# Delta rule in packed 32x32 blocks for all chunks at once, differential attention kept in flight, fox tails last

## The chip, the cores and the metric

The kernel runs on one core of a Trainium2 chip. The metric is the device time of one execution in microseconds (us): the median of three runs. One more execution was taken by the hardware profiler; all rows below are of that one. The engines are PE (TensorE, the matrix engine; PEld is its weight load), DVE (VectorE), ACT (ScalarE), POOL (GpSimd) and SP (SyncE, which only issues transfers). Each has its own instruction queue and works through it in order; they wait for each other by semaphores. PE reads SBUF and writes PSUM, which has 8 banks of 128x512 numbers. Everything is computed in 32-bit floats; a 32-bit matmul appears in the trace as two PE instructions, a transpose as one.

## The reference, cut to what matters

Four layers on 512 tokens (528 with 16 meta tokens) of width 1024: an even layer (pooling and differential attention), an odd layer (latent attention and the gated delta rule), a forgetting ("fox") attention with a mixture of experts, and a gated recurrence ("hg") with a second mixture of experts. The change touches three of them.

```python
def diff_attention(q, k, v, lam):            # 6 heads, two maps of depth 64 each, causal
    s = einsum('bqhmd,bkhmd->bhmqk', qb, k) * scale
    pr = softmax(where(mask, s, -inf))
    a = pr[:, :, 0] - lam * pr[:, :, 1]
    return einsum('bhqk,bkhe->bqhe', a, v)   # then rmsnorm(o, subln) * (1 - lam_init) * silu(b_gate)

dq = l2norm(dq) * DK_D ** -0.5; dk = l2norm(dk)          # 4 heads of 128
def gated_delta_rule(q, k, v, g, beta):
    gc = cumsum(g)                                        # inside each chunk
    gamma = exp(where(incl, gc[..., :, None] - gc[..., None, :], -inf))
    a_mat = eye + where(strict, (k @ k.T) * gamma * beta[..., :, None], 0)
    u, w = triangular_solve(a_mat, [v * beta, k * beta * exp(gc)])
    qk = (q @ k.T) * gamma
    for each chunk:                                       # S is 128x128 per head
        v_new = u - w @ S
        o = (q * exp(gc)) @ S + qk @ v_new
        S = S * exp(gc_last) + (k * exp(gc_last - gc)).T @ v_new

# fox attention: 16 heads of 64; scores plus differences of cumulated forget gates, causal, softmax, times v
```

## The kernel before

The program is a chain of stages, each a block in which every engine has its own list; an engine enters the next block when its own list is done and the others are. Where this text names a line as L373, it is that line of the kernel; L373 is the helper `products`, which records a sum of matmuls for many stages.

**Even input** (`stage_even_in`): PE makes 36 units of eight matmuls, ACT and DVE empty the banks, POOL rotates the heads.

**Even attention** (`stage_even_attention`): 24 jobs (t, h), four query tiles t of 128 by six heads. A job has keys of width 128(t+1). PE makes two maps of scores (L780, depth 64) and adds the causal mask to each by a matmul with the identity (L781); DVE takes the row maximum (L880) and scales it (L882); ACT takes the exponential out of PSUM with its sum (L844); DVE inverts the sums, scales the first map (L893) and adds the second (L895); PE transposes the result (L789), ACT copies it (L835), PE multiplies it by the values (L373), DVE copies that out (L903). Scores of job j+1 stand ahead of the transposes of job j, and have to wait until the exponentials of job j-1 have read their bank. After six heads DVE squares, sums, normalises and gates the row tile (L908 to L916), with the root on POOL (L279, L281, L283), and PE turns it (L805). The pooling of the even layer (POOL L710 to L731, two matmuls, DVE L745) stands in the same stage.

**Odd input** (`stage_odd_in`): units of eight matmuls in the order low, cgate, conv (12), small (8 columns), dgate. DVE makes the convolution of each conv unit (L1048 to L1053), ACT its silu (L1019).

**Delta rule** (`stage_delta`): first a block that transposes all twelve channel groups (L1387), takes the norms of queries and keys per token on DVE and POOL (L1446 to L1450) and turns them back (L1396), then makes the log gates. Then a second block goes over four chunks of 128 tokens, one after the other, each with its four heads side by side: masks and decays (L1628 to L1640), then the inverse of the unit triangular matrix by doubling: at levels 1 to 6 PE makes L*T (L1531), DVE copies it (L1647), PE makes U*X and X*U (L1537, L1540), DVE masks the next level (L1650) and subtracts (L1654, L1658); T and U are the inverse and its transpose, 128x128 for each head. Then the scan step (L1546 to L1563), and for each chunk a root and two products on POOL (L1609, L1611) and a transpose (L1517).

**Fox attention** (`stage_fox_attention`): jobs of one list; first four "tail" jobs (four heads each, 16 queries), then 32 "pair" jobs (two heads, query tile t). PE: scores (L1926, L1928; for tails L1917, L1918), then the transposes of the job three back (L1944; L1938, L1940), then the products of the job four back (L1965; L1956, L1957). DVE adds the gate row and takes the minimum in one instruction (L2038), ACT takes the exponential in place (L1998), POOL scales by the inverted sum (L2016). SP loads gate rows for later jobs and then zeroes the expert rows in memory (`zero_expert_rows`).

`inverse_root` (POOL L275 to L283) serves all norms. `stage_hg` builds its 32x32 masks from the constants by 24 small copies (L3016), and multiplies blocks of 32 columns (L2712).

## Time and profile before

| | us |
|---|---|
| median of three runs | 3334.73 (3331.75 to 3338.49) |
| profiled execution, its own time | 3341.96 |
| its span, first to last instruction | 3340.1 |
| PE busy | 2668.4 (80%) |
| DVE busy | 871.8 (26%) |
| ACT busy | 498.9 (15%) |
| POOL busy | 448.6 (13%) |
| even attention, 232.5 to 426.3 | 193.8 |
| odd input, 599 to 754.5 | 155.5 |
| delta rule, 895.5 to 1123.4 | 227.9 |
| fox attention, 1472.0 to 1598.1 | 126.1 |

The span is that of the instructions; 1.9 us of the execution's time lie around it. Busy shares are averages over stages that are bound by different things. PE is busy in four fifths of the span, but a busy matmul record is not a full array: the records overlap and their ends are modelled. What counts is the distance between starts. "PEclk" is the share of 2.4 GHz that was granted; 0.50 means 1.2 GHz.

### The profile page before, as it was taken

How to read it: one execution, taken by the hardware profiler on the slowest of the kernel's cores; microseconds unless marked ns; L12 is line 12 of the kernel's file. 1: busy time of each engine (PE TensorE's matmuls, PEld its weight loads, DVE VectorE, ACT ScalarE, POOL GpSimd, SP SyncE). 2: the span in 40 equal slices, each digit the busy share in tenths (PEclk: the TensorE clock that was granted, in tenths of full speed). 3: DMA queues.
4: the chain of work that ended last, by engine and by line, in shares of the span. 5: the costliest groups of instructions: out<-in, count | busy, mean ns of one | idle time of the engine just before them, and what ended most of it. 6: DMA issues, size and time to landing. Idle time of an engine off the chain costs nothing. (4 is left out here: it accounts for less than half of the span.)

```text
span 3340.1 us, 31732 instructions
## 1 busy us (share of the span) xinstructions
PE 2668.4 (80%) x12346; PEld 1339.6 (40%) x12346; DVE 871.8 (26%) x1847; ACT 498.9 (15%) x1154; POOL 448.6 (13%) x681
## 2 busy tenths in 40 slices
PE   6988888995757898999838777775989875777774
PEld 3654444452556544456432222222435442222221
DVE  2315411124366213205131110103055422101111
ACT  1102101012300002115100000001134300000000
POOL 1510001006010002217110000002044200000001
PEclk9995599997778999989959999997989887998987
DMA  4220012102000004203349999995101035999997
GB/s 148 76 91 1 0 54 76 51 16 91 1 1 1 26 8 147 76 8 120 143 195 367 416 415 417 415 416 172 36 27 52 26 153 220 415 417 415 416 415 289
DMA packets 196225, 570.13 MB, mean 171 GB/s; under 512 B 21040, under 2 KB 31152, under 8 KB 195984
## 3 DMA queue, kind: packets, MB, share of 16 engines
q1 hardware_dynamic: 181136, 534.77, 41.0%
q0 software_dynamic: 4736, 17.04, 1.4%
q10 hardware_dynamic: 10240, 16.79, 1.4%
q8 instruction: 74, 1.21, 0.1%
q14 instruction: 39, 0.32, 0.0%
HBM read 524.23 MB, written 44.21 MB: 170 GB/s over the span
## 5 line engine op out<-in xcount | busy, mean ns | idle before, releaser
L373 PE MATMUL psum<-weight_ring,hidden_T 128*128 128x512 f32 (+3 forms) x1792 | 714.1, 557 | 14.5 <-DMA arena<-in_p_T 10.4
L373 PEld LDWEIGHTS psum<-weight_ring,hidden_T 128*128 128x128 f32 x1792 | 339.0, 194 | 364.8 <-issue 290.6
L2381 PE MATMUL psum<-weight_ring,hidden_T 128*64 128x512 f32 x1024 | 284.0, 717 | 102.8 <-DMA weight_ring<-in_moe_w_up 95.9
L2393 PE MATMUL psum<-weight_ring,hidden_T 128*64 128x512 f32 x1024 | 233.8, 599 | 30.3 <-ACT hidden_T L2439 30.3
L2381 PE MATMUL psum<-arena,hidden_T 128*64 128x512 f32 x1024 | 230.0, 602 | 27.1 <-DMA arena<-in_moe_w_up 27.0
L2381 PEld LDWEIGHTS psum<-weight_ring,hidden_T 128*64 128x64 f32 x1024 | 94.5, 164 | 272.0 <-issue 257.1
L2455 DVE TENSOR_TENSOR hidden_T<-hidden_T,psum 128x256 f32<-128x256 f32 x64 | 27.0, 422 | 603.4 <-ACT hidden_T L2437 603.4
L2563 POOL DMA_INDIRECT arena<-expert_rows_out,arena x18 | 21.3, 1185 | 1067.8 <-PEq L2552 1062.9
L275 POOL TENSOR_SCALAR arena<-arena 128x1 f32<-128x1 f32 (+5 forms) x97 | 20.9, 215 | 941.5 <-ACT arena L1091 186.6
L2381 PEld LDWEIGHTS psum<-arena,hidden_T 128*64 128x64 f32 x1024 | 71.8, 138 | 184.6 <-issue 132.8
L2393 PEld LDWEIGHTS psum<-weight_ring,hidden_T 128*64 128x64 f32 x1024 | 67.8, 136 | 155.1 <-issue 109.6
L2437 ACT ACTIVATE hidden_T<-psum 128x256 f32<-128x256 f32 x64 | 24.5, 383 | 692.9 <-PE psum L2381 692.9
L2685 PE MATMUL psum<-weight_ring,hidden_T 128*128 128x512 f32 x256 | 123.4, 612 | 0.0
L2459 DVE COPY arena<-psum 128x512 f32<-128x512 f32 x64 | 44.3, 692 | 301.7 <-PE psum L2393 301.7
L373 PE MATMUL psum<-hidden_T,weight_ring 128*128 128x512 f32 (+2 forms) x288 | 119.4, 576 | 3.5 <-PEq L298 3.5
L373 PE MATMUL psum<-weight_ring,arena 128*128 128x512 f32 (+1 forms) x240 | 115.8, 629 | 2.1 <-PEq L2662 1.0
L2677 PE MATMUL psum<-hidden_T,weight_ring 128*128 128x512 f32 x256 | 111.4, 595 | 3.8 <-PEq L298 1.8
L365 PE MATMUL psum<-constants,arena 128*128 128x128 f32 (+1 forms) x216 | 40.2, 363 | 82.2 <-ACT arena L325 80.7
L279 POOL TENSOR_TENSOR arena<-arena,constants 128x1 f32<-128x1 f32 (+5 forms) x89 | 94.9, 1066 | 7.4
L2368 PE MATMUL psum<-constants,hidden_T 128*128 128x128 f32 x256 | 36.7, 289 | 65.0 <-DMA hidden_T<-expert_rows_in 65.0
L373 PE MATMUL psum<-arena,hidden_T 128*128 128x36 f32 (+2 forms) x264 | 61.8, 413 | 30.9 <-PEq L298 18.3
L457 DVE TENSOR_TENSOR hidden<-hidden,psum 128x512 f32<-128x512 f32 (+1 forms) x34 | 23.4, 687 | 221.4 <-PE psum L373 220.8
(461 smaller groups left out, 3169.9 us busy)
## 6 DMA issues: line engine op xcount, KB each, us to landing
weight_ring<-in_moe_w_up SPq DMA_DIRECT2D x32, 4096.0 KB, 23.3
weight_ring<-in_moe_w_down SPq DMA_DIRECT2D x64, 2048.0 KB, 24.0
arena<-in_moe_w_up SPq DMA_DIRECT2D x32, 4096.0 KB, 25.5
hidden_T<-expert_rows_in SPq DMA_DIRECT2D x32, 512.0 KB, 19.9
expert_rows_out<-arena ACTq DMA_DIRECT2D x128, 128.0 KB, 5.5
weight_ring<-in_hg_w_in SPq DMA_DIRECT2D x8, 2048.0 KB, 8.8
weight_ring<-in_ev_w_in SPq DMA_DIRECT2D x8, 1536.0 KB, 6.7
weight_ring<-in_fox_w_in SPq DMA_DIRECT2D x6, 2048.0 KB, 8.5
```

The source lines that it names most:

```text
L279: g.nc.gpsimd.tensor_tensor(out, out, power, ALU.pow).then_inc(*done.up())
L365: last = nc.tensor.transpose(g.psum[:, 2 * (i % 2) + c // 4, (c % 4) * P:(c % 4) * P + n], src, g.c("identity")[0:n, 0:n])
L373: last = nc.tensor.matmul(out, l, r, start=i == 0, stop=i == len(left) - 1)
L457: nc.vector.tensor_tensor(dst, dst, g.psum[0:n, u % 4, :], ALU.add).then_inc(*added.up())
L2368: last = nc.tensor.transpose(g.psum[:, c // 4, (c % 4) * P:(c % 4 + 1) * P], x[:, c // 4, (c % 4) * P:(c % 4 + 1) * P], g.c("identity"))
L2381: last = nc.tensor.matmul(g.psum[64 * q:64 * q + 64, 2 + n, :].rearrange("p (s c) -> p s c", s=2), xT[:, k // 4, k % 4, ROWS * n:ROWS * n ...
L2393: last = nc.tensor.matmul(g.psum[64 * q:64 * q + 64, 6 + n, :], aT[:, k % 2, 64 * (k // 2):64 * (k // 2) + 64], down[n][:, k, 512 * q:512 ...
L2437: nc.scalar.activation(s, g.psum[:, 2 + n, 0:256], ACT.Silu).then_inc(silu.sem, 1)
L2455: nc.vector.tensor_tensor(act_, s, g.psum[:, 2 + n, 256:512], ALU.mult).then_inc(hid.sem, 1)
L2459: nc.vector.tensor_copy(y[n], g.psum[:, 6 + n, :]).then_inc(y_placed.sem, 1)
L2677: last = mm(bank(u % 2), w[:, k, (x % 4) * P:(x % 4 + 1) * P], g.hT[:, k, META:], **flags)
L2685: last = mm(bank(u % 2), g.hT[:, k, a:a + n], w[:, k, :], **flags)
```

## The change

**Even attention.** The mask is no longer a matmul: DVE adds a strip of constants and takes the minimum of the negated scores in one instruction and writes them to SBUF (three buffers), ACT takes the exponential in place, so a bank of scores is free once DVE has read it. The division moves behind the product with the values: POOL multiplies the second map by one coefficient and adds it to the first, and DVE scales the 128 columns of the result. PE's list is scores of job j, transposes of j-2, values of j-3. ACT squares the rows head by head, POOL multiplies the gates by the gain at the stage's start. The pooling windows, the lambda and the gains move into the even input stage.

**Odd input.** The order becomes low, small, conv, cgate, dgate. ACT squares each query and key channel group, PE sums it over channels by four matmuls with a column of ones, and the log gates, their sums and all row scales are made here.

**Delta rule.** One block. Queries and keys are used as they stand, channels first, and the norms enter as row scales. All four chunks' decays are built first (POOL builds two operands for each chunk, PE spreads them, ACT takes exponentials). The inverse is then taken for all 16 (chunk, head) matrices at once: their 32x32 diagonal blocks are packed, in two halves of 8 matrices, and levels 1 to 4 work on those blocks alone; levels 5 and 6 join them by blocks of 32 and 64. The scan works with the residual (v - k*S) instead of two solved right sides.

**Fox attention.** The tails stand behind the pairs. **Constants.** Seven masks of 128 columns are replaced by one of 192, and the pooling factors are loaded in the even input stage.

```diff
+    c["masks"] = np.tile(np.concatenate([pairs(1 << n) for n in range(5)] + [np.eye(32)], 1), (4, 1))
...
+        self.const = sb("constants", [P, const_at["pool"][0]])
...
+            pool.wait_ge(*freed_a.at(2))
+            pooling.windows(pool)
...
                 if j >= 2:
-                    if 2 * (j - 1) > 0:
-                        pe.wait_ge(*expd.at(2 * (j - 1)))
+                    pe.wait_ge(*peaked.at(2 * (j - 2) + 2))
                 for m in range(2):
                     r = slice(64 * m, 64 * m + 64)
-                    bank = g.psum[:, 2 * (j % 2) + m, :]
-                    nc.tensor.matmul(bank[:, 0:cw(t)], g.e_qT[r, h, t * P:(t + 1) * P], g.e_kT[r, h, 0:cw(t)], start=True, stop=False)
-                    nc.tensor.matmul(bank[:, t * P:cw(t)], g.c("identity"), g.c("causal"), start=False, stop=True).then_inc(*scored.up())
-
-            def mix(j):
+                    nc.tensor.matmul(g.psum[:, 2 * (j % 2) + m, 0:cw(t)], g.e_qT[r, h, t * P:(t + 1) * P], g.e_kT[r, h, 0:cw(t)], start=True, stop=True).then_inc(*scored.up())
...
+            pooling.products(pe)
+            for j in range(N + 10):
+                if j < N:
+                    scores(j)
+                if 2 <= j < N + 2:
+                    turn(j - 2)
+                if 3 <= j < N + 3:
+                    if j == 3:
+                        pe.wait_ge(*pooling.done.at(2))
+                    values(j - 3)
+                if j >= 13 and (j - 13) % HB in (0, 2):
+                    turn_rows((j - 13) // HB, (j - 13) % HB // 2)
...
+                gate = hv(g.e_bg[:, t, :])
+                nc.gpsimd.tensor_tensor(gate, gate, subln.unsqueeze(1).to_broadcast([P, HB, DVB]), ALU.mult).then_inc(*gated.up())
+            for j in range(N + 9):
+                if j < N:
+                    t, h = jobs[j]
+                    pool.wait_ge(*inverted.at(j + 1))
+                    a = sc[:, j % 3, 0, 0:cw(t)]
+                    b = sc[:, j % 3, 1, 0:cw(t)]
+                    nc.gpsimd.tensor_scalar(b, b, coef[:, j % 3:j % 3 + 1], None, ALU.mult).then_inc(*gchain.up())
+                    pool.wait_ge(*gchain.last())
+                    nc.gpsimd.tensor_tensor(a, a, b, ALU.add).then_inc(*combined.up())
+                if j >= 10 and (j - 10) % HB == 0:
+                    t = (j - 10) // HB
+                    if t < 4:
+                        pool.wait_ge(*squared.at(HB * (t + 1)))
+                        inverse_root(g, pool, so[:, t % 2, :], so[:, t % 2, :], 1.0 / DVB, gchain, rooted)
 
...
+                    v.tensor_tensor_reduce(out=sc[:, j % 3, m, 0:cw(t)], in0=g.psum[:, 2 * (j % 2) + m, 0:cw(t)], in1=strip[:, SEQ - cw(t):], scale=1.0, scalar=3e38,
+                                           op0=ALU.add, op1=ALU.min, accum_out=peak[:, j % 3, m:m + 1]).then_inc(*peaked.up())
...
+                v.reciprocal(inv[:, j % 6, :], total[:, j % 3, :]).then_inc(*chain.up())
                 dve.wait_ge(*chain.last())
-                v.tensor_tensor(total[:, j % 2, 1:2], total[:, j % 2, 1:2], lam[:, 0:1], ALU.mult).then_inc(*chain.up())
...
+            def head_sums(f):
+                pe.wait_ge(*squared.at(f + 1))
+                if f == 0:
+                    pe.wait_ge(*cum_read.at(2))
+                for t in range(4):
+                    last = nc.tensor.matmul(stats[:, 4 * f + t:4 * f + t + 1], sq[:, f % 2, t * P:(t + 1) * P], ones, start=True, stop=True)
+                last.then_inc(*summed.up())
...
             def decays(n):
+                pe.wait_ge(*built.at(2 * n + 2))
+                if n >= 2:
+                    pe.wait_ge(*exped.at(4 * (n - 1)))
+                mm(pq(4 + n % 2), ones, up_gl[n % 2], start=True, stop=False)
+                mm(pq(4 + n % 2), g.c("identity"), g.c("later").unsqueeze(1).to_broadcast([P, HD, P]), start=False, stop=True).then_inc(*cumd.up())
+                if n < 2:
+                    pe.wait_ge(*valued.at(2 * n + 2))
+                else:
+                    pe.wait_ge(*paired.at(3 * (n - 1)))
+                for h in range(HD):
+                    mm(pair(2 * (n % 2))[:, h, :, :], kT(h, n), g.o_conv[:, h:h + 5:4, n * P:(n + 1) * P], start=True, stop=True)
+                mm(pq(6 + n % 2), ones, id_bk[n % 2], start=True, stop=True).then_inc(*keyed.up())
...
+            def lower(x, n):
+                if n < 6:
+                    pe.wait_ge(*ts.at(2 * (n - 1) + x + 1))
+                if n < 5:
+                    pe.wait_ge(*masked.at(3 * x + 3 if n == 1 else 6 + 2 * (n - 2) + x + 1))
+                    for q in range(8):
+                        for i in range(4):
+                            last = mm(blocks(bank(x, n), 32)[rows(i), q, :], Lv[x][n % 2][rows(i), q, :], Tc[rows(i), 8 * x + q, :], start=True, stop=True)
+                elif n == 5:
+                    for q in range(8):
+                        for a in (0, 2):
+                            last = mm(blocks(bank(x, n), 32)[rows(a + 1), q, :], LT[rows(a), 8 * x + q, rows(a + 1)], Tc[rows(a), 8 * x + q, :], start=True, stop=True)
+                else:
+                    pe.wait_ge(*lows.at(2 * x + 2))
+                    for q in range(8):
+                        last = mm(blocks(bank(x, n), 64)[64:128, q, :], LT[0:64, 8 * x + q, 64:128], lo[0:64, 8 * x + q, :], start=True, stop=True)
+                last.then_inc(*level_prod.up())
+            def left(x, n):
+                pe.wait_ge(*xs.at(nth(x, n)))
+                pe.wait_ge(*(us.at(nth(x, n - 1)) if n > 1 else masked.at(3 * x + 2)))
+                for q in range(8):
+                    for i in range(4) if n < 5 else (1,):
+                        last = mm(blocks(other(x, n), 32)[rows(i), q, :], Uc[rows(i), 8 * x + q, :], Xc[rows(i), 8 * x + q, :], start=True, stop=True)
+                last.then_inc(*t_prod.up())
+            def right(x, n):
+                pe.wait_ge(*xs.at(nth(x, n)))
+                for q in range(8):
+                    if n < 5:
+                        for i in range(4):
+                            last = mm(blocks(bank(x, n), 32)[rows(i), q, :], Xc[rows(i), 8 * x + q, :], Uc[rows(i), 8 * x + q, :], start=True, stop=True)
...
+            for h in range(HD):
+                turn(h, 8 + h)
             for n in range(NCH):
+                decays(n)
+            first(0)
+            turn_keys(0)
+            first(1)
+            turn_keys(1)
+            for n in range(1, 7):
+                lower(0, n)
+                if n > 1:
+                    right(1, n - 1)
+                else:
+                    turn_keys(2)
+                if n < 6:
+                    left(0, n)
+                lower(1, n)
+                right(0, n)
+                if n == 1:
+                    turn_keys(3)
+                if n < 6:
+                    left(1, n)
+            solve(0, 0)
+            solve(0, 1)
+            right(1, 6)
+            for n in range(NCH):
                 if n:
+                    by_state(n)
+                    solve(n, 0)
+                    solve(n, 1)
                 if n + 1 < NCH:
+                    update(n, 0)
+                    update(n, 1)
+                mix(n)
+                if n:
+                    turn_rows(n - 1)
...
-    jobs = [("tail", n, 0) for n in range(TAILS)] + [("pair", p, t) for p in range(FH // 2) for t in range(4)]
+    jobs = [("pair", p, t) for p in range(FH // 2) for t in range(4)] + [("tail", n, 0) for n in range(TAILS)]
...
-    job_of = lambda p, t: TAILS + 4 * p + t
+    job_of = lambda p, t: 4 * p + t
```

On PE, in even attention, one step of the list in the last query tile stood as follows before (L780 and L781 scores and mask, L789 transposes, L373 values):

```order
L780 MATMUL psum<-arena 128x512
L781 MATMUL psum<-constants 128x128
L780 MATMUL psum<-arena 128x512
L781 MATMUL psum<-constants 128x128
L789 MATMUL psum<-constants,arena 128x128 x4
L373 MATMUL psum<-arena,hidden_T 128x128 x4
```

and now (L805 scores, L813 transposes, L373 values):

```order
L805 MATMUL psum<-arena 128x512 x2
L813 MATMUL psum<-constants,arena 128x128 x4
L373 MATMUL psum<-arena 128x128 x4
L805 MATMUL psum<-arena 128x512 x2
L813 MATMUL psum<-constants,arena 128x128 x4
L373 MATMUL psum<-arena 128x128 x4
```

The two mask matmuls are gone and the two maps of scores stand next to each other; what stands behind them belongs to jobs two and three back, not one and two.

On PE, in the delta rule, two levels of one chunk stood as follows before:

```order
L1531 MATMUL psum<-arena 128x128 x4
L1537 MATMUL psum<-arena 128x128 x4
L1540 MATMUL psum<-arena 128x128 x4
L1531 MATMUL psum<-arena 128x128 x4
L1537 MATMUL psum<-arena 128x128 x4
L1540 MATMUL psum<-arena 128x128 x4
```

and now, for all four chunks, the end of level 4 and the two joins (L1564 and L1568 are the first product of a join, L1576 the one for the inverse, L1584, L1587 and L1591 the one for its transpose, L1620 the first use of the result):

```order
L1576 MATMUL psum<-arena 32x32 x32
L1564 MATMUL psum<-arena 32x32 x16
L1584 MATMUL psum<-arena 32x32 x32
L1576 MATMUL psum<-arena 32x32 x8
L1564 MATMUL psum<-arena 32x32 x16
L1587 MATMUL psum<-arena 32x32 x16
L1576 MATMUL psum<-arena 32x32 x8
L1568 MATMUL psum<-arena 64x64 x8
L1587 MATMUL psum<-arena 32x32 x16
L1568 MATMUL psum<-arena 64x64 x8
L1591 MATMUL psum<-arena 64x64 x8
L1620 MATMUL psum<-arena 128x128 x4
```

Where there were four matmuls of 128x128 for each chunk and product, there are now 32 (in the joins 16 or 8) small ones for each half and product, and the halves alternate. Over the stage the list has 912 matmuls of 32x32 and 32 of 64x64.

On PE, in the odd input stage, the sums over channels now stand between the conv units:

```order
L1041 MATMUL psum<-arena,constants 128x16
L1042 MATMUL psum<-arena,constants 128x16
L373 MATMUL psum<-hidden_T,weight_ring 128x512 x8
L1021 MATMUL psum<-constants,arena 128x1 x4
L373 MATMUL psum<-hidden_T,weight_ring 128x512 x8
L1021 MATMUL psum<-constants,arena 128x1 x4
```

Eight groups of four such matmuls of one column are added to the stage.

## Rows read from the trace of the kernel before

**Rows 1.** Windows: stage, us, busy (count) of PE PEld DVE ACT POOL, PEclk, DMA, GB/s

```profile
232.50:426.30 193.80, 154.56 (x400) 88.91 (x401) 96.63 (x251) 38.89 (x123) 21.25 (x26) 0.52 0.05 18
599.00:754.50 155.50, 154.65 (x398) 73.53 (x396) 34.04 (x53) 17.85 (x32) 0.00 (x0) 0.97 0.11 36
895.50:942.00 46.50, 16.42 (x80) 12.53 (x80) 20.52 (x27) 11.87 (x19) 10.64 (x20) 0.58 0.00 0
942.00:1123.40 181.40, 130.50 (x905) 120.22 (x905) 114.20 (x189) 12.44 (x53) 18.93 (x20) 0.86 0.00 1
1472.00:1598.10 126.10, 116.30 (x980) 82.41 (x980) 55.48 (x221) 55.37 (x173) 75.08 (x70) 0.89 0.34 120
```

**Rows 2.** Timeline of ACT in even attention: start, us, instruction, idle and releaser

```profile
255.77 0.37 ACT L844 ACTIVATE arena<-psum,arena 128x128 f32<-128x128 f32 x1 [2.45 <-DVE arena L882]
260.29 0.37 ACT L844 ACTIVATE arena<-psum,arena 128x128 f32<-128x128 f32 x1 [2.45 <-DVE arena L882]
```

**Rows 3.** Timeline of PE in the last query tile of even attention

```profile
374.74 2.05 PE L373 MATMUL psum<-arena,hidden_T 128*128 128x128 f32 x8 [0.41 <-DVE arena L903]
```

**Rows 4.** Timeline of PE in fox attention, first at half clock, then at full

```profile
1500.57 0.64 PE L1956 MATMUL psum<-arena 128*64 128x16 f32 x8
1503.69 2.08 PE L1926 MATMUL psum<-arena 64*128 64x512 f32 x4
...
1541.09 1.13 PE L1926 MATMUL psum<-arena 64*128 64x512 f32 x4
...
1550.16 1.04 PE L1944 MATMUL psum<-constants,arena 128*128 128x128 f32 x8
1551.93 1.13 PE L1926 MATMUL psum<-arena 64*128 64x512 f32 x4
...
1554.88 0.49 PE L1926 MATMUL psum<-arena 64*128 64x128 f32 x4
```

**Rows 5.** Groups by form in fox attention: xcount, busy us, mean ns, idle before

```profile
L2016 POOL TENSOR_SCALAR arena<-arena 128x512 f32<-128x512 f32 x10 | 15.5, 1563 | 2.8 <-DVE arena L2044 2.8
L2038 DVE CUSTOM_DVE_ANT_0 arena<-psum,arena 128x512 f32<-128x512 f32 x10 | 6.5, 688 | 12.3 <-PE psum L1928 12.3
L2016 POOL TENSOR_SCALAR arena<-arena 128x128 f32<-128x128 f32 x10 | 5.9, 603 | 6.8 <-DVE arena L2044 6.8
```

**Rows 6.** Timeline of POOL: before even attention, a product, a product by a broadcast

```profile
232.79 0.31 POOL L710 MEMSET arena<- 128x256 f32 x1 [77.74 <-POOLq L554]
...
945.69 4.93 POOL L1602 TENSOR_TENSOR arena<-arena 128x512 f32<-128x512 f32 x4 [12.11 <-DMA arena<-in_od_o_norm]
1118.90 1.04 POOL L1609 TENSOR_TENSOR arena<-arena 128x512 f32<-128x512 f32 x1
```

**Rows 7.** Timeline of PE in one chunk's inverse, one level and the next

```profile
966.58 1.16 PE L1537 MATMUL psum<-arena 128*128 128x128 f32 x8 [0.94 <-DVE arena L1647]
967.58 1.06 PE L1540 MATMUL psum<-arena 128*128 128x128 f32 x8
970.62 1.16 PE L1537 MATMUL psum<-arena 128*128 128x128 f32 x8 [0.94 <-DVE arena L1647]
```

**Rows 8.** Timeline of PE in the hg stage, products of 32 columns

```profile
2442.18 0.66 PE L2712 MATMUL psum<-weight_ring 128*32 128x32 f32 x32 [15.79 <-DVE weight_ring L2956]
2442.77 6.01 PE L2685 MATMUL psum<-weight_ring,hidden_T 128*128 128x512 f32 x10
2448.71 0.46 PE L2712 MATMUL psum<-weight_ring 128*32 128x32 f32 x32
2449.10 4.56 PE L2685 MATMUL psum<-weight_ring,hidden_T 128*128 128x512 f32 x10
```

**Rows 9.** A window, and one group by form (713.5 to 716 us) in odd input

```profile
719.00:721.00 2.00, 2.00 (x11) 2.00 (x11) 0.17 (x1) 0.00 (x0) 0.00 (x0) 0.50 0.00 0
...
L373 PE MATMUL psum<-weight_ring,hidden_T 128*128 128x8 f32 x20 | 2.3, 252 | 0.0
```

**Rows 10.** Timeline of DVE at the start, and the transfer of the constants (KB, us to landing)

```profile
14.26 0.17 DVE L228 CAST arena<-arena 128x4 f32<-128x4 int32 x1 [14.26 <-DMA hidden<-in_meta_tokens]
...
constants<-in_constants SPq DMA_DIRECT2D x1, 1664.5 KB, 6.8
```

943 lines of the change are left out of this document (527 added, 416 removed).

## The prediction

> **What bounds the kernel now.** I read the windows by stage first, then the timeline of each changed stage, then the groups of the stages that already hold the new kind of work. Half of the time lies in the experts and hg and is not touched. In [rows 1] the four touched stages take 193.8, 155.5, 227.9 (46.5 and 181.4) and 126.1 us. Three are bound by different things.
>
> Even attention is a chain of waits with one job in flight, on a slow PE: the granted clock is 0.52 [rows 1], that is 1.2 GHz nearly throughout. In [rows 2] ACT's exponential of two following jobs of the first tile stands 4.52 us apart, 2.45 of it waiting for DVE's L882; DVE waits for PE's mask, PE for ACT to free the bank. Odd input is PE alone (154.65 of 155.5 busy). The delta rule's inverse is a chain PE, DVE, PE, DVE with PE idle 0.94 us in each level of 4.04 us (966.58 to 970.62, [rows 7]); six levels, four chunks, one after the other, about 97 us. Its first 46.5 us hold 16.4 us of PE and 20.5 of DVE [rows 1]: norms and turns, everyone waiting. In fox attention pairs run at PE's pace, 10.84 us for four jobs (1541.09 to 1551.93, [rows 4]), 8 times that is 86.7 of the 126.1 us; the rest is start, tails and drain.
>
> **Even attention, part by part.** Gone: two mask matmuls, two L882, the scaling of one map, and the wait of scores for exponentials. New: POOL scales and adds a map. PE's order is scores j, transposes j-2, values j-3; so transposes of job j start when POOL has combined it, and POOL starts when DVE has done the peaks of job j+1 and the inversion. That loop spans two jobs: twice the period is scores, two peaks, inversion, POOL, transposes, values and some five hops of 0.1.
> Last tile, full clock: scores 1.06 (both maps side by side, start to start in [rows 4]: 1.13 recorded), peaks 2 x (0.69 + 0.08) = 1.54 [rows 5], inversion 0.35 (two tiny DVE operations), POOL 1.56 [rows 5] + 1.04 [rows 6] = 2.6, four transposes half of 1.04 [rows 4], values 0.9, hops 0.5: 7.5, so 3.7 a job. First tile: 0.42 + 0.75 + 0.35 + 0.9 + 0.13 + 0.25 + 0.5 = 3.3, 1.65 a job. Mean 2.7, times 24 is 65 us. At half clock scores take 2.0 [rows 4], values 2.05 [rows 3], transposes 1.04: 10.1 or 5.05 a job, first tile 2.0; mean 3.5, 85 us. POOL itself (2.7 a job in the last tile) and DVE (2.3) stay under either. Which clock: the two maps now fill the array's rows together, as in fox pairs, but PE has under 60% work at full clock. I take 75. Ahead of the first combination POOL has four gate products of 768 columns, 1.5 x 1.23 each [rows 6]: 7.4, with the first job 9. Row tiles cost DVE two passes of 768 columns, 1.03 each by the 0.69 for 512 [rows 5], that hold up the next peaks at three of four tile ends, partly behind POOL: 4. The drain (copy, values, square, root, two passes, two turns): 12. Stage 100, gain 94 (bounds 75 at half clock with 5 of new waits, 112). The pooling windows move into even input, at whose end POOL is idle for 77.74 us [rows 6]: nothing; without that cover their dozen products of about 1.1 would cost 13.
>
> **Odd input.** 32 matmuls of one column. The nearest are 8 columns wide: 20 instructions in 2.3 us at full clock [rows 9], 0.23 a matmul; at 719 to 721, at half clock, 11 instructions fill 2 us, 0.36 a matmul. Between dense units I take 0.23: 7.4, and the two gate sums make 8 (bounds 6 and 13). ACT gets a square of about 0.6 (and six table loads over the stage) in units of 16 instructions of 0.43, 6.9: hidden.
>
> **Delta rule.** The first block goes (46.5). New, in PE's order:
> Building: three matmuls of 512 and four of 256 columns for each chunk, at 0.45 an instruction of 512 (10 in 4.56, [rows 8]): 4.5, four times is 18; with 16 transposes 21. POOL feeds it with two products of 1.23 a chunk, so it isn't late. The second half's masks come after the last scores on DVE, four ACT copies and two POOL products: PE waits about 5 there. Key turns 2.
> Blocks: in [rows 8] 32 instructions, 16 matmuls, take 0.59 us after a pause (2442.18 to 2442.77) and 0.39 at full clock: 37 and 24 ns a matmul. Such sparse work I expect at half clock, since 8-column matmuls pull it down although PE is busy throughout [rows 9]; 912 x 0.037 = 34. The 32 of 64x64 at about 0.15: 5. A half's own chain in a level (product 1.2, copy 0.4, product 1.2, subtraction 0.4, hops) is 3.6 against 7.1 of PE work for both, so levels are PE's; only the two joins wait, 5.
> Scan: 20 matmuls of 128x128 a chunk at 0.24 (8 instructions in about 1.0, [rows 7]) 4.8, and `turn_rows(n - 1)` stands in front of the next chunk's first product, so DVE's 8 row scalings of 0.3 after `mix` are on the path: 8 a chunk, three of them 24, first chunk 3, end 4, half clock at its start 5: 36.
> Sum 21 + 5 + 2 + 34 + 5 + 5 + 36 = 108, gain 120. Bounds: 90 (24 ns, no mask wait, full clock), 142 (build at half clock 42, scan 45, rest 55): gains 138 and 86.
>
> The Trainium skill says otherwise of small products: "TensorE: Matmul & The Clock Gate", section "Wait — 56ns, not 53.3ns?", has the sequencer spend about 62 ns on each MATMUL with hardware decoding off. Then 944 x 2 x 62 ns is 117 us where I have 39, and the gain in this stage would be 42. [Rows 8] show 18 ns an instruction at the worse of the two, so this case's trace does not agree, though there all blocks read 128 rows.
>
> **Fox and the start.** With tails last: first turn after 3.6, pairs 86.7, then four tails. A tail's 16-column products are sixteen matmuls, four in 0.64 at a low clock [rows 4]; so 2.6, with four shorter ones 0.5, transposes 0.7 and scores 1.0 it is 4.8 a tail, up to 7.7 where the clock halves; 6.5, since this work pulls the clock down: 26. The end 2, and the output stage starts at half clock, 1.7. Together 120 for 126: gain 6 (bounds -3 and 15). Zeroing memory is issued as far before the end as now and lands beside the output stage; if the dense output weights were not already loaded it would show. The constants lose 1728 columns, 0.88 MB, and DVE starts at 14.26 when the loads have landed [rows 10]: at some 400 GB/s, 2. The mask copies of hg lie beside its weights' matmuls: nothing.
>
> **Sum.** 94 - 8 + 120 + 6 + 2 = 214 off the profiled execution's 3341.96, so 3128. That execution lies 7.2 over the median, so 3120.7, in round numbers 3120.
>
> **Rivals.**
> A. The clock stays at half in even attention, the building and the scan. For it: 0.52 in the whole stage now [rows 1], at 80% busy. Against: fox pairs at 1.00, with the same side-by-side scores. It costs 10 + 21 + 10 and about 5 at the edges: 3166.
> B. Better: full clock, few waits, blocks at 24 ns: even attention 88, delta 92: 3120 - 12 - 16 - 5 = 3087, near 3070 if fox gives 15 as well.
> C. Blocks cost an instruction of their own, as the rule above has it: 3120 + 78 = 3198. For it: nothing here has 32 rows and 32 columns at once. Against: [rows 8].
> D. Slower than now: tile products on four row groups do not overlap, and each waits for its own weights, as the 8-column matmuls do: 0.36 us each [rows 9]. The place is levels 1 to 6; 944 x 0.36 = 340 where I have 39: 3120 + 301 = 3421. It decides from (39 + 214) / 944 = 0.27 a matmul. The 16-column products of [rows 4], 0.16 each on one tile, stay under that: + 112, 3232.
> E. The change doesn't do what it says in even attention: PE, which takes everything in order, waits for POOL each time and the period stays near that of now, say 5.5 mean: + 60, 3180.
>
> **Chances.** Forecast 0.60, A 0.12, B 0.12, C 0.05, D 0.03 (0.16 each instead: 0.03), E 0.05. The forecast is the likeliest. The range reaches to B and past A and E: 3055 to 3190, leaving C and D out. Faster by over 0.2% (6.7 us, about what a measurement of this kernel tells from no change): 0.96; within 0.2%: 0.01; slower: 0.03.
>
> **What would show it.** Even attention: jobs of the last tile 3.5 to 5 us apart, PE waiting for POOL's sum, ACT never waiting for a bank; if scores wait for peaks instead, the loop is named wrongly. Odd input 8 longer, with no PE idle between conv units. Delta: 32 block matmuls start to start about 1.2 us; over 2 is C, over 8 is D; one visible PE idle before the second half's first product, and one before each chunk's first product in the scan, released by DVE through the turn. Fox: clock full from the second pair, half in the tails. Wrong altogether if a stage not named here moves by over 5 us.

## The result, and the profile after

The changed kernel takes 3135.76 us in the median of four runs (3133.49 to 3138.48), the kernel before 3336.61 (3331.75 to 3348.73): ratio 0.9388, interval 0.9368 to 0.9408. The forecast was 3120, range 3055 to 3190. So the direction and the range hold, and 16 us of gain are missing. The profiled execution took 3137.03, 9 more than the 3128 of my sum. The rest of the 16 is no stage's: I took the median to lie 7.2 under the profiled execution, as before the change, and this time it lies 1.3 under it.

By stage, from PE's first instruction of one stage to that of the next (before, after, in us; the last column is my forecast; the windows of [rows 1] are cut by hand and differ from these by up to 1.4 us):

| stage | before | after | change | forecast |
|---|---|---|---|---|
| start, norm, even input | 232.5 | 228.4 | -4.1 | -2 |
| even attention | 193.8 | 94.0 | -99.8 | -94 |
| its output, ple | 173.2 | 177.3 | +4.1 | 0 |
| odd input | 154.1 | 164.5 | +10.4 | +8 |
| MLA | 142.2 | 138.9 | -3.3 | 0 |
| delta rule | 227.6 | 122.5 | -105.1 | -120 |
| output to fox input | 348.6 | 349.3 | +0.7 | 0 |
| fox attention and output | 192.3 | 186.5 | -5.8 | -6 |
| all behind | 1675.8 | 1673.8 | -2.0 | 0 |

The windows that answer to [rows 1] (stretch, length, busy and count of PE, PEld, DVE, ACT, POOL, then PE's granted clock, DMA, GB/s); of the delta rule first the building, then blocks, scan and the whole:

```profile
228.40:322.40 94.00, 62.19 (x305) 40.61 (x305) 50.37 (x186) 45.42 (x169) 61.38 (x60) 0.78 0.10 34
499.70:664.20 164.50, 160.67 (x457) 79.99 (x455) 36.55 (x71) 34.31 (x53) 5.66 (x2) 0.96 0.13 47
803.10:829.20 26.10, 22.07 (x140) 14.77 (x140) 11.59 (x18) 7.74 (x24) 14.06 (x16) 0.90 0.02 4
829.20:887.90 58.70, 36.08 (x1821) 32.90 (x1821) 11.79 (x27) 10.57 (x26) 9.24 (x11) 0.56 0.02 4
887.90:925.50 37.60, 27.21 (x168) 25.09 (x168) 15.60 (x52) 13.68 (x56) 4.82 (x8) 0.77 0.00 0
803.10:925.50 122.40, 85.36 (x2128) 72.76 (x2128) 38.98 (x97) 31.99 (x106) 28.12 (x34) 0.70 0.01 3
1274.90:1393.30 118.40, 112.80 (x980) 80.40 (x981) 55.50 (x221) 55.23 (x173) 75.20 (x70) 0.92 0.35 123
```

Read the fourth line first. In the blocks' 58.7 us PE is busy for 36.1, and no other engine for more than 12. The waits of PE in 35 us of it, levels 2 to 4 (839 to 874 us; line, released by, us in all, times, longest) name no engine:

```profile
PE psum L1576 <- issue: 7.1, 4, 1.9
PE psum L1584 <- issue: 6.6, 3, 2.5
PE psum L1560 <- issue: 6.1, 3, 2.1
```

"Issue" is idle time in which PE waited for nothing that the profile shows: 19.8 us in 35. The timeline of PE says where it falls:

```profile
850.37 0.58 PE L1576 MATMUL psum<-arena 32*32 32x32 f32 x25 [1.40 <-issue]
850.72 1.08 PE L1560 MATMUL psum<-arena 32*32 32x32 f32 x64
851.57 0.73 PE L1584 MATMUL psum<-arena 32*32 32x32 f32 x38
854.47 0.58 PE L1584 MATMUL psum<-arena 32*32 32x32 f32 x26 [2.17 <-issue]
854.82 1.09 PE L1576 MATMUL psum<-arena 32*32 32x32 f32 x64
855.67 0.72 PE L1560 MATMUL psum<-arena 32*32 32x32 f32 x37
858.44 0.58 PE L1560 MATMUL psum<-arena 32*32 32x32 f32 x26 [2.05 <-issue]
```

Two things are to be seen. A group of 32 products (64 instructions here, as many weight loads beside them) runs in 0.85 us, 27 ns a product, once it runs. And PE stops in the middle of a group, between two products with no semaphore wait between them, after 25 + 64 + 38 = 127 and 26 + 64 + 37 = 127 recorded instructions, with the weight loads about 256. In the same window, 840 to 880 us, the queue that brings instructions shows 11 packets (queue, kind: packets, MB, share):

```profile
q8 instruction: 11, 0.18, 2.1%
```

That is 16 KB each and one for every stop: the eleven packets of the trace start 1.1 to 1.3 us behind PE's eleven restarts from 839.24 to 877.50 (at 851.60, 855.73 and 859.49 for the restarts at 850.37, 854.47 and 858.44), 3.8 us apart on the average. By the share, 2.1% of 16 engines' 40 us, a packet takes 1.2 us. Over the kernel the queue has 82 packets and 1.34 MB, before 74 and 1.21. Hence the theory that the experiments test, F: PE's instructions arrive 256 at a time, a load comes 3.3 to 4.1 us after the one before (3.86 on the average of the nine from 839.24 to 873.94), and products that are done sooner wait for it (the expectations call 256 instructions a page). The rivals: Q, each small product costs PE some 61 ns of its own; R, the chain of PE, VectorE and ACT sets the levels and the records hide it.

### The profile page after: what moved, and what is told of

It is laid out like the page before. It is cut to its first block and busy times, and to the rows that moved or that the text cites. A ratio compares the mean times of both kernels' runs of the same rounds, so it can differ in the third digit from the quotient of the medians.

```text
span 3135.2 us, 33847 instructions
## 1 busy us (share of the span) xinstructions
PE 2516.5 (80%) x13462; PEld 1235.8 (39%) x13462; DVE 728.6 (23%) x1664; ACT 530.3 (17%) x1258; POOL 506.8 (16%) x727
## 3 DMA queue, kind: packets, MB, share of 16 engines
q8 instruction: 82, 1.34, 0.2%
## 5 line engine op out<-in xcount | busy, mean ns | idle before, releaser
L373 PE MATMUL psum<-weight_ring,hidden_T 128*128 128x512 f32 (+3 forms) x1792 | 711.2, 555 | 15.1 <-DMA arena<-in_p_T 11.4
L373 PEld LDWEIGHTS psum<-weight_ring,hidden_T 128*128 128x128 f32 x1792 | 337.8, 194 | 363.6 <-issue 288.4
L2621 PE MATMUL psum<-weight_ring,hidden_T 128*64 128x512 f32 x1024 | 275.4, 699 | 96.5 <-DMA weight_ring<-in_moe_w_up 89.5
L2633 PE MATMUL psum<-weight_ring,hidden_T 128*64 128x512 f32 x1024 | 233.9, 598 | 30.3 <-ACT hidden_T L2679 30.3
L373 PE MATMUL psum<-hidden_T,weight_ring 128*128 128x512 f32 (+2 forms) x288 | 124.5, 589 | 3.3 <-PEq L298 3.3
L373 PE MATMUL psum<-weight_ring,arena 128*128 128x512 f32 (+1 forms) x240 | 117.6, 636 | 3.1 <-DVE hidden_T L1311 1.1
L275 POOL TENSOR_SCALAR arena<-arena 128x1 f32<-128x1 f32 (+6 forms) x90 | 20.3, 225 | 608.3 <-ACT arena L313 157.9
L279 POOL TENSOR_TENSOR arena<-arena,constants 128x1 f32<-128x1 f32 (+6 forms) x90 | 102.1, 1134 | 7.5
L2256 POOL TENSOR_SCALAR arena<-arena 128x128 f32<-128x128 f32 (+3 forms) x64 | 68.4, 1087 | 78.6 <-DVE arena L2284 78.6
## 6 DMA issues: line engine op xcount, KB each, us to landing
hidden_T<-expert_rows_in SPq DMA_DIRECT2D x32, 512.0 KB, 19.8
```

Source lines behind the costliest of these rows:

```text
L279: g.nc.gpsimd.tensor_tensor(out, out, power, ALU.pow).then_inc(*done.up())
L373: last = nc.tensor.matmul(out, l, r, start=i == 0, stop=i == len(left) - 1)
L2256: nc.gpsimd.tensor_scalar(s, s, total[:, j % 4, m:m + 1], None, ALU.mult).then_inc(*normed.up())
L2621: last = nc.tensor.matmul(g.psum[64 * q:64 * q + 64, 2 + n, :].rearrange("p (s c) -> p s c", s=2), xT[:, k // 4, k % 4, ROWS * n:ROWS * n ...
L2633: last = nc.tensor.matmul(g.psum[64 * q:64 * q + 64, 6 + n, :], aT[:, k % 2, 64 * (k // 2):64 * (k // 2) + 64], down[n][:, k, 512 * q:512 ...
```

## The experiments

Each is an edit of the changed kernel, timed against the kernel before on the same chip in five rounds, the one with two dense products in three. "Stage" is read off the profiled execution, since the total of one and the same kernel moves by some us with the clock. The unchanged kernel was timed in the first series only, with the three runs named next to it below (one dense product, fewer instructions, gate sums). The four last runs are of a second chip and the one with two dense products of a third; the kernel before took 3343.50, 3342.05 and 3339.30 us on the three, so a difference of theirs from the unchanged kernel is across chips. The unchanged kernel in this series showed odd input 3 us longer than above, and the delta rule at 122.4.

**Unchanged, as the measure.** 

> The changed kernel as it is, as the measure for the others on the same chip: 3136 us, ratio 0.939 of the kernel before. Every theory says so; a stage that moves by over 1 us against the first profile of it shows how far stages can be compared between executions.

Measured: 3133.24 us (3131.93 to 3135.75), ratio 0.9369 (0.9355 to 0.9382).

**One dense product ahead of each group of block products.**

```diff
             def lower(x, n):
+                fill(n)          # and in left, right; acts for n = 2 to 4
...
+            def fill(n):
...
+                mm(pq(5), g.c("identity"), vb[:, 0, :, :], start=True, stop=True)
```

> In levels 2 to 4 of the delta rule's inverse one 512-column product of its own (its result is not used) is put ahead of each group of 32 block products, 18 in all, about 0.9 us each at full clock and 1.8 at half: 15 to 32 us of additional PE work. Theory F (the stretch is paced by the supply of PE's instructions, 256 of them, weight loads counted, every 3.9 us, of which PE stands idle for 2.0): the products fall into the idle time, the 72 added instructions cost 1.1 us, stage 122.5 to at most 126, total within 4 us of the changed kernel. Theory Q (each small product occupies PE or its queue for about 61 ns, the idle time in the records is none): the work comes on top, 15 us or more. Theory R (a chain of PE, DVE and ACT steps sets a level): the products delay the chain, since PE takes them in order: 10 us or more.

Measured: the stage is 122.2 us, against 122.4. Eighteen products of 512 columns cost nothing. Total 3139.40, ratio 0.9392 (0.9376 to 0.9407); the profiled execution is 3.7 us longer than the unchanged one, and these lie behind the stage, 2 of them in hg. Window and timeline of PE:

```profile
844.00:859.00 15.00, 14.11 (x528) 7.82 (x528) 2.11 (x5) 0.93 (x3) 5.53 (x5) 1.00 0.02 5
859.00:874.00 15.00, 14.43 (x550) 7.74 (x550) 2.19 (x6) 0.99 (x3) 0.00 (x0) 1.00 0.02 4
...
868.21 1.12 PE L1557 MATMUL psum<-arena,constants 128*128 128x512 f32 x2
869.26 0.75 PE L1567 MATMUL psum<-arena 32*32 32x32 f32 x64
869.95 1.13 PE L1557 MATMUL psum<-arena,constants 128*128 128x512 f32 x2
871.00 0.75 PE L1593 MATMUL psum<-arena 32*32 32x32 f32 x64
```

PE is now busy for 14.1 to 14.4 of 15 us, at a granted clock of 1.00 where it had 0.50, and the pace of the groups has not moved. Idle time by issue over levels 2 to 4 falls from 19.8 to 3.8 us. So neither the half clock nor a cost of each product set the pace. Q would have added 15 us or more. The stops that are left have moved with the count and still fall inside groups: one after 24 instructions of a group (853.88, the next starts at 854.68), 127 recorded instructions behind the stop before it, and one after 15 of another (861.65, the next at 862.05), 255 behind that. A chain of the other engines, R, would stop PE at a group's start, where its semaphore waits are. This also answers what my forecast made of the clock: it called for 37 ns a product because the clock would be at half. Half it was, and it made no difference.

**Two dense products ahead of each group.** The same with a second line `mm(pq(4), ...)`.

> As the run with one 512-column product ahead of each of the 18 groups, but with two (the results are not used). Theory F: with one of them a group and its product took 1.74 us and a page of 256 instructions about 3.4, so that only 0.2 us of idle time a page was left. The second, 0.86 to 1.05 us, finds no room: group and products 2.6 to 2.8 us, the 18 take 47 to 50 us where they take 33 to 35 now, stage 122.2 to 136 or 139 and the idle time by issue gone. The first was free, the second is paid in full. Theory R' (the products were free only because a chain of other engines had slack of its own): the second is partly free as well, stage under 130.

Measured: 3139.91 us, ratio 0.9401 (0.9378 to 0.9424). PE's timeline:

```profile
852.09 1.13 PE L1557 MATMUL psum<-arena,constants 128*128 128x512 f32 x2
853.05 1.02 PE L1558 MATMUL psum<-arena,constants 128*128 128x512 f32 x2
854.01 0.75 PE L1568 MATMUL psum<-arena 32*32 32x32 f32 x64
854.69 1.13 PE L1557 MATMUL psum<-arena,constants 128*128 128x512 f32 x2
```

A group with its two products takes 2.60 us, nearly each time, and idle time by issue is 0.2 us in all. From the start of the first of these groups to that of the last it is 45.6 us (838.10 to 883.73), where it was 34.9 in the unchanged kernel of the series and, with one product each, 34.5. So the first product is free and the second is paid, as F has it: 17 of the second products stand in that stretch, some 14.6 us, of which 11 were paid and the rest went into the 3.8 that one product had left. The stage grew less than I expected, to 129.2 and not 136, for a reason that I had not counted: what stands behind gave 4.6 us back, since there were fewer stops in the joins and the first 64x64 products now ran at full clock (16 instructions in 1.14 us, not 1.97). By my own line "under 130 is R'" the number falls on the wrong side. Nor does a PE that is busy throughout tell F from R', which would end in the same; what R' has no place for are stops inside a group at equal counts.

**Fewer instructions: VectorE makes one factor from the other.** The two factors kept are transposes of each other in each 32x32 block. Ten groups of 32 products go.

```diff
-            first(0) ... first(1) ...                  # 2 groups of 32; the rest of the list alternates the halves
-                right(1, n - 1) ... right(0, n)        # 8 groups, levels 1 to 4
 (VectorE)
-                v.tensor_copy(Tc[:, eight(x), :], blocks(bank(x, 0), 32))
+                v.transpose(Tc[:, eight(x), :], Uc[:, eight(x), :])
-                    v.tensor_tensor(u, u, blocks(bank(x, n), 32), ALU.subtract)
+                    v.transpose(Uc[:, eight(x), :], Tc[:, eight(x), :])
```

> VectorE's transpose of 32x32 blocks makes the one factor of the inverse from the other, in place of the first two and eight later groups of 32 block products and their subtractions: 320 products or 1280 PE instructions fewer, 10 VectorE operations of another kind in place of 10, and the two halves' groups alternate. Theory F (supply of instructions): 5 pages of 256 fewer at 3.9 us, -19 us (-16 to -22), levels 7.8 us each where they take 11.7. Theory Q (61 ns for each product): -19.5 too. Theory R (the chain of steps sets a level): a transpose is added to each half's chain, so no gain, +-3 us; a gain of 5 to 12 would say that supply and chain take turns. By my recorded 37 ns a product the gain would be 12.

Measured: the stage is 103.1 us, -19.3. Total 3117.45 (3113.55 to 3122.14), ratio 0.9325 (0.9311 to 0.9339), 15.8 under the unchanged one. Theory F gave -19 (and Q, which the dense products had ruled out, the same), R nothing. Stops are still there, after the same number of instructions and now at every second group:

```profile
841.24 1.38 PE L1570 MATMUL psum<-arena 32*32 32x32 f32 x86 [1.50 <-issue]
...
844.67 1.40 PE L1554 MATMUL psum<-arena 32*32 32x32 f32 x89 [1.51 <-issue]
845.87 0.73 PE L1570 MATMUL psum<-arena 32*32 32x32 f32 x38
848.10 1.44 PE L1570 MATMUL psum<-arena 32*32 32x32 f32 x90 [1.50 <-issue]
```

89 + 38 = 127 again. From 834.11 to 855.79 the restarts are 3.43 to 3.98 us apart, 3.61 on the average, where it was 3.86 in the changed kernel (839.24 to 873.94 in nine, 3.33 to 4.10 each). Why a load takes now less and now more stays open. VectorE's transpose (128x256) takes 0.45 us, the subtraction that it replaces 0.42.

**Odd input: copy the gate sums one unit earlier.** In the changed kernel PE's first head sums wait for VectorE, which empties their bank only behind the taps of the fourth unit (PE's timeline, then a window):

```profile
532.67 7.11 PE L373 MATMUL psum<-hidden_T,weight_ring 128*128 128x512 f32 x16
543.61 1.52 PE L1021 MATMUL psum<-constants,arena 128*128 128x1 f32 x8 [3.83 <-DVE arena L1128]
544.99 9.99 PE L373 MATMUL psum<-hidden_T,weight_ring 128*128 128x512 f32 x16
554.82 0.95 PE L1021 MATMUL psum<-constants,arena 128*128 128x1 f32 x8
...
543.60:552.00 8.40, 8.39 (x18) 4.46 (x19) 0.15 (x2) 0.63 (x1) 0.00 (x0) 0.59 0.39 147
```

```diff
...
-                elif f == 4:
+                elif f == 3:
                     cum = g.o_decay.rearrange("p n t h -> p n (t h)")
```

> In odd input VectorE copies the cumulated gates out of the statistics bank before the taps of the fourth conv unit, not of the fifth, so that PE's first head sums don't wait for it (3.83 us idle at 539.8 in the changed kernel, then 8.4 us at a granted clock of 0.59, which cost about 3 more). If that wait and its clock are what my odd input term lacked: the stage 164.5 to about 158, total -6 to -7 us. Rival: PE would wait at the second sums instead, or ACT falls behind: 0 to -2 us. Rival: only the idle time goes and the clock was going to fall anyway: -3.8.

Measured: no wait is left, PE is busy for 159.07 of the stage's 159.1 us (499.7 to 658.8), where it took 164.5 and, in the unchanged run of this series, 167.5. So -5.4 to -8.4 in the stage, and 5.0 above the 154.1 of before. The total says less: 3130.73 (3117.90 to 3135.53), ratio 0.9351 (0.9330 to 0.9373), 2.5 under the unchanged kernel and within the intervals. In the profiled executions MLA behind it took 133.7 us against 130.2, which gives 3.5 of it back; the two spans differ by 3.5.

**The scan: row turns off the path.**

```diff
+                if n >= 2:
+                    turn_rows(n - 2)       # behind solve(n, 1)
                 ...
                 mix(n)
-                if n:
-                    turn_rows(n - 1)
-            turn_rows(NCH - 1)
+            turn_rows(NCH - 2)
+            turn_rows(NCH - 1)
```

with VectorE's scalings and ACT's copy of a chunk moved back in the same way.

> In the delta rule's scan the row turn, its row scalings on VectorE and its copy on ACT come one chunk later, behind the next chunk's solve, in place of ahead of its first product. If the turn stands on the path, as I had it (PE idle 2.26 us for L1891 and 0.9 of turn in each chunk of 9.1 and 8.7 us): a chunk becomes products by the state, rests, solve, copy, update, state, 6.2 to 6.5 us by the rows of the changed kernel; two chunks give 2.5 each, the first pair of turns that now stands at the end costs 2: stage 122.4 to about 118, total -4 (-2 to -7). Rival: VectorE's other work (row scalings in place of the wait) sets the chunk anyway: 0, or 2 slower at the end.

Measured: the stage is 116.2 us, -6.2, at the far end of what I gave. PE's products by the state (L1602) follow each other in 5.7 us, where they took 8.2 and 8.8; first the changed kernel, then this one:

```profile
902.64 1.12 PE L1644 MATMUL psum<-constants,arena 128*128 128x128 f32 x4 [2.26 <-DVE arena L1891]
903.54 1.91 PE L1602 MATMUL psum<-arena 128*128 128x128 f32 x8
...
911.80 0.66 PE L1644 MATMUL psum<-constants,arena 128*128 128x128 f32 x4 [2.27 <-DVE arena L1891]
912.29 1.63 PE L1602 MATMUL psum<-arena 128*128 128x128 f32 x8
```

```profile
906.54 1.06 PE L1602 MATMUL psum<-arena 128*128 128x128 f32 x8
...
910.00 0.66 PE L1644 MATMUL psum<-constants,arena 128*128 128x128 f32 x4 [0.32 <-DVE arena L1895]
...
912.28 1.06 PE L1602 MATMUL psum<-arena 128*128 128x128 f32 x8
```

The total doesn't show it: 3130.77 (3129.99 to 3139.89), ratio 0.9375 (0.9358 to 0.9393), against 0.9369. In the profiled execution MLA attention ran slow, 59.9 us where it took 54.5.

**Even attention: VectorE combines the maps.**

```diff
 (VectorE, behind the inversion)
+                v.scalar_tensor_tensor(a, b, coef[:, j % 3:j % 3 + 1], a, ALU.mult, ALU.add).then_inc(*combined.up())
...
 (POOL)
-                    nc.gpsimd.tensor_scalar(b, b, coef[:, j % 3:j % 3 + 1], None, ALU.mult).then_inc(*gchain.up())
-                    nc.gpsimd.tensor_tensor(a, a, b, ALU.add).then_inc(*combined.up())
```

> In even attention VectorE combines the two maps in one scalar_tensor_tensor after its inversion; POOL keeps only the gate products and the roots. Theory L (a loop over two jobs, scores, two peaks, inversion, POOL's two passes of 1.57 and 1.27 us, turns, values, sets the period of 3.7 us in the last tile): without POOL the loop is 5.0 us for two jobs and VectorE's own 2.95 a job (two peaks 1.5, inversion 0.4, the pass 0.7, the take 0.35) sets it, -0.7 a job over the three wider tiles and -3 where the first combination waits behind POOL's gate products: stage 94 to about 83, total -10 (-6 to -14). Theory V (VectorE or PE's order is the bound already): the pass adds to VectorE, +0.5 a job, 5 to 12 slower.

Measured: the stage is 71.6 us, -22.4; total 3115.15 (3108.26 to 3120.73), ratio 0.9325 (0.9306 to 0.9345), 18 under the unchanged kernel (15 by the ratios). Theory L holds, and I undersized it (-6 to -14 was my range): the last tile's period falls from 3.96 to 2.90 us, but the second tile's from 3.2 to 2.1 and the third's from 3.6 to 2.7. Two things that I had left out are in the traces: POOL's roots (1.35 us in one operation, once a tile) also stood between two of its sums, and the granted clock of the stage rises from 0.78 to 0.91. How the 22.4 divide between them wasn't measured. Waits of PE in the stage, changed kernel and this one, and its window:

```profile
PE psum L813 <- POOL arena L885: 25.5, 18, 3.9
PE psum L828 <- DVE arena L924: 4.0, 1, 4.0
```

```profile
PE psum L813 <- ACT arena L862: 8.3, 15, 1.5
PE psum L828 <- DVE arena L920: 5.8, 4, 4.2
...
228.60:300.20 71.60, 52.46 (x305) 33.80 (x305) 61.56 (x210) 44.88 (x169) 11.95 (x12) 0.91 0.12 45
```

VectorE is busy for 61.6 of 71.6 us now; that it sets the pace is likely and wasn't tested.

**Fox attention in the order of before.** `jobs`, `job_of`, the order of the loads and the tails' bank go back; nothing else.

> Fox attention alone in the order of before (the four tail jobs first, their transfers, their bank 7), all else of the changed kernel kept. If the order is the whole of the stage's change: 118.4 back to 126.1, total +7.7, of which I had forecast 6. Rival: part of the 7.7 came from the clock that the stages ahead leave behind: +3 to +5. In the end of the stage I expect the output stage's first 3.6 us at half clock to go back to full, -1.7.

Measured: 3150.71 (3148.17 to 3153.92), ratio 0.9430 (0.9414 to 0.9445), 17 slower than the unchanged kernel. The stage takes 132.7 us, 14.2 over the 118.4 with the tails last; both of my numbers, +7.7 and +3 to +5, missed that. The output stage behind it came back to 66.2 us, as expected. With the very order of before the stage is 6.6 longer than before, so the order isn't the whole of it. Windows of this run, and of the same stretch of the tails before:

```profile
1290.00:1305.00 15.00, 15.00 (x89) 11.98 (x89) 2.52 (x12) 2.95 (x10) 1.36 (x3) 0.50 0.01 2
1305.00:1320.00 15.00, 15.00 (x94) 12.34 (x94) 1.73 (x7) 2.09 (x6) 4.10 (x4) 0.50 0.13 36
```

```profile
1488.00:1503.00 15.00, 15.00 (x103) 12.10 (x102) 2.52 (x12) 3.35 (x10) 3.00 (x4) 0.59 0.01 2
1503.00:1518.00 15.00, 15.00 (x110) 10.87 (x111) 4.49 (x20) 4.29 (x15) 6.72 (x6) 0.77 0.10 36
```

Here the clock is at half throughout the tails, from 1281.3 to 1322.2, and comes back 48 us into the stage; before, it was back for part of both windows, and for good 42 us into the stage. That is 40.9 us at half against 27.3; an estimate from these, half of the difference, is 6.8 us, and 6.6 were measured. The tails' 16-column products, four in 1.04 us at 0.50, take 0.64 at 1.00.

**The four together.** Transposes, later row turns, early gate sums, VectorE's combination.

> The changed kernel with VectorE's transposes in the inverse, the later row turns in the scan, the early copy of the gates in odd input and VectorE's combination in even attention. Measured or expected alone: stages -19.3, -4, -6.6, -10. They lie in different stages or one behind the other, so they should add: 3133 - 40 = 3093 (3085 to 3105). Rival: the clock takes part back behind each shortened stage, as behind odd input (the next stages 2.9 slower): 3105 to 3115.

Measured: 3088.04 us (3081.79 to 3091.03), ratio 0.9236 (0.9221 to 0.9252), 45 under the changed kernel, within the 3085 to 3105 that I gave, though the four stages alone had gained 53 to 56 in all. Part of that was taken back elsewhere, as my rival had it: in the profiled execution MLA took 5.5 us more than in the unchanged kernel (its attention 58.8 us, at a granted clock of 0.82), and all behind the fox layer 3 more. Even attention takes 71.6 us again, the delta rule 97.6, and odd input has no wait:

```profile
513.70:638.10 124.40, 124.40 (x341) 59.06 (x339) 28.75 (x51) 27.37 (x42) 5.66 (x2) 1.00 0.08 28
781.30:878.90 97.60, 73.53 (x1488) 62.30 (x1489) 38.58 (x97) 31.74 (x106) 28.06 (x34) 0.73 0.01 3
```

## Why the prediction was right, and where it was wrong

**Even attention, -94 forecast, -99.8.** The mechanism is the one named: PE takes everything in order, waits for POOL's sum (18 times), and the loop spans two jobs: PE's turns in the last tile start 7.5, 7.2, 7.8 and 7.5 us after the last but one (285.45, 289.07, 292.92, 296.31, 300.71, 303.76). I had 7.5 at full clock, and from 285 to 310 us the granted clock was 0.97. ACT never waits for a bank. I was 5.8 too careful, some 4 of them at the start: POOL's four gate products take 6.06 us and the first sum comes 5.2 us after the first scores, where I had 9. The bounds that I gave, gains of 75 and 112, don't come out of my own terms: half clock with 5 us of waits makes a stage of 115 and a gain of 79, full clock one of 90 and a gain of 104.

**Odd input, +8, +10.4.** The 32 products cost a little less than I said (four in 0.80 us, where I had 0.92). What I said would not happen did: PE idle between units, for 3.83 us, and a clock of 0.59 behind it. Taking this wait away gave 5.4 us or more and leaves the stage 5.0 over that of before, so that my +8 came near the 10.4 by luck: too much for the products, nothing for the wait. I looked for VectorE's and ACT's load, and not for what PE's added instruction waits on in VectorE's order of work.

**Delta rule, -120, -105.1: the step that failed.** Building without its wait 21 against 20.8; the wait of the second half's masks 5 against 4.07; scan 36 against 37.6. The block term is the one that was mis-sized: blocks, 64x64 products, joins and key turns were 46 and came to 60. I took 37 ns a product from [rows 8], and it costs 60 on the average of the levels (64 products in 3.86 us), 1.93 us for a group of 32, just under the 2 that I had set as C's sign. [Rows 8] were the right form and the wrong surroundings: there 16 small products stand between dense ones, and the trace shows no stop among them (the packets of instructions are 16 us apart there, 2443.40 and 2459.72). In a long row of them the supply falls behind. The run with one fill shows that this, and neither the clock nor the product, is the price, and the run with 1280 instructions fewer shows its size. Half clock, which I had given as the reason for the 37 ns, did come (0.50), but it wasn't what set the pace.

Rival C had 62 ns for each of two instructions of a product, 117 us for them all. The trace does not agree: an instruction takes 13 ns while they run. That the average is 60 ns a product comes from the stops.

The Trainium skill has the mechanism: "Runtime: NRT & Kernel Launch", section "Instruction fetch mechanics", says that each engine's instruction memory is refilled in blocks of 16 KiB, 256 instructions, by a queue of the sequencer, and that crossing a block's border is "mostly hidden". The trace agrees with the block, 127 or 128 products' and as many loads' instructions between stops. It does not agree that it is hidden: 19.8 us of 35 in levels 2 to 4.

**Fox and the start, -6 and -2; -5.8 and -4.1.** Fox attention 118.4 where I had 118.3, and the output stage 1.9 longer from half clock where I had 1.7. My tail term rested on a misread row: the 0.64 us of [rows 4] that I took for a low clock was at full clock (1.00 from 1500.5 to 1503.0), and at half it is 1.04; that I then took 6.5 a tail, between 4.8 and 7.7, made up for it. In the tails the first runs at full and the rest at half clock:

```profile
1370.24 0.64 PE L2196 MATMUL psum<-arena 128*64 128x16 f32 x8
...
1374.63 1.04 PE L2196 MATMUL psum<-arena 128*64 128x16 f32 x8
```

But the run in the old order shows that the value of the reordering isn't a constant: 7.7 us against the kernel before, 14.2 against the same code behind other stages. Tails in front lose more when the clock stays down longer. Of the start, VectorE's first instruction comes at 11.63 for 14.26 [rows 10], -2.6; the rest came and went with the clock of the norm in other executions.

**What I did not name.** No other stage moved by over 5 us, as said, but +4.1 behind even attention and -3.3 in MLA are in these traces. The latter goes with the clock: MLA attention, the same code, ran at 0.82 before and 0.91 after. The cause of the former stays open: the clock was 0.95 before and 0.94 after, and in the unchanged run of the series the stage took 174.8, not 177.3.

```profile
748.90:803.10 54.20, 48.63 (x233) 31.84 (x234) 20.67 (x68) 16.53 (x49) 0.05 (x1) 0.91 0.00 1
```

In the other runs it took 54 to 55 or 59 to 60 us with the same code. Of the rivals, A (half clock in even attention, building and scan) didn't come: 0.78, 0.90 and 0.77, and near half only in the first half of even attention (0.63 up to 248 us, 0.59 from there to 267); E's wait for POOL comes each time, but in the loop that the sum already had. B's 24 ns came near for a group (27) and not for a row of groups, and D's tiles that don't overlap would have taken 11.5 us a group of 32, not 0.85.

That the total is only 9 us off in the profiled execution is in part luck: 14.9 us of gain that didn't come in the delta rule and 2.4 of added cost in odd input stand against 5.8 in even attention and 2.1 at the start that I hadn't forecast, and these are of other causes.

## What to carry to other kernels

Count instructions, not only their durations: where PE's are short (32-column products with their loads), a stretch took 3.3 to 4.1 us for every 256 of them here, and the sign of it in a profile is idle time by "issue" in the middle of a group, at equal counts. Dense work placed there is free, up to the idle time; work that another engine can do in one instruction is worth moving. And before a duration is taken from rows elsewhere in the trace, look at what stands around it there.

When an engine gets a new instruction, follow what that instruction waits for to the place in the other engine's order where it is signalled; that wait, of 3.8 us and more with its clock, was in the order of work and in no duration.

## What the runs showed of the hardware

- PE's instruction supply: stops of 1.4 to 2.5 us after about 127 recorded product instructions (and as many weight loads), one 16 KB packet of the instruction queue for each, 3.61 us apart on the average in one kernel and 3.86 in another.
- 64 product instructions of 32x32 blocks on four row groups follow each other in 0.85 us at a granted clock of 0.50 and in 0.56 at 1.00 (839.45 to 840.01 in the changed kernel), while each is recorded as lasting some 0.2 us: the tiles overlap. Over a row of groups the stops take back what the clock gives.
- A dense product of 512 columns ahead of each such group lifts the granted clock from 0.50 to 1.00.
- VectorE's transpose of 32x32 blocks (128x256, from SBUF to SBUF, 0.45 us) stands in for 32 products and a subtraction, and PE's stops by issue were still there in the levels.
- One stage with the same code but for one clearing of memory on POOL took 126.1 and 132.7 us, another 54 and 59, by when the clock came back. Comparisons of a few us have to be made by stage.
